# RWKV scan in an encoder kernel: a chunk's state share accumulates in the bank of the passed-on share, and the second direction's decay products move up beside it

## The reference, cut to what matters

```
def step(state, inp):                       # one token; state is 64 x 64 for each head
    r, w, k, v, a, b = inp
    sa = state @ a
    state = state * w + outer(sa, b) + outer(v, k)
    return state, state @ r
out = scan(forward inputs) + flip(scan(flipped inputs))
w = exp(-exp(w_log)),  icl = sigmoid(a0 + ad @ a_up),  w_log = -softplus(-(w0 + wd @ w_up)) - 0.5
```

## Time and profile before

| | us |
|---|---|
| median of 3 runs | 1811.07 (1809.88 to 1813.27) |
| the profiled execution | 1806.79 |
| its span, first to last instruction | 1805.1 |
| TensorE busy with matmuls | 1633.4 |
| VectorE busy | 1235.8 |
| ScalarE busy | 769.1 |
| mean granted TensorE clock, share of full | 0.946 |

### The profile page before, as it was taken

One profiled execution on the slowest core, in us unless ns is written; L12 is line 12 of the kernel. 1 busy time (PEld: TensorE's weight loads), 2 busy tenths in 40 slices (PEclk: granted clock), 3 DMA queues, 4 the chain that ended last, 5 costly groups with the idle time before them and its releaser, 6 DMA issues.

```text
span 1805.1 us, 43648 instructions
## 1 busy us (share of the span) xinstructions
PE 1633.4 (90%) x17117; PEld 1507.3 (84%) x17117; DVE 1235.8 (68%) x1850; ACT 769.1 (43%) x1163; POOL 92.4 (5%) x112
## 2 busy tenths in 40 slices
PE   6999998868878889999999999988688788999999
PEld 6999986757868869999889988867588687899997
DVE  5677667897647556777666777678874665567766
ACT  5444553435232135544444446534342311355444
POOL 1000100001100001000000002000011000010000
PEclk9999998978979989999999999989689799999999
DMA  5755532222102025555556554222220121355555
GB/s 187 263 181 184 173 106 71 94 94 71 38 25 84 27 81 165 178 187 178 189 195 227 187 185 166 94 71 95 70 85 25 36 72 38 102 165 180 187 183 192
DMA packets 62927, 231.58 MB, mean 128 GB/s; under 512 B 7024, under 2 KB 8048, under 8 KB 61840
## 3 DMA queue, kind: packets, MB, share of 16 engines
q1 hardware_dynamic: 61488, 221.41, 36.4%
q0 software_dynamic: 1248, 7.46, 1.1%
HBM read 228.09 MB, written 1.05 MB: 127 GB/s over the span
## 4 chain that ended last, share of the span: by engine, by line
PE 70%; DVE 14%; issue 9%; ACT 5%; DMA 2%; DVEq 0%; ACTq 0%; SPq 0%; POOLq 0%
PE banks L538 14%; PE banks L540 13%; PE banks L539 13%; PE banks L605 9%; PE banks L606 5%; DVE wlo L1407 3%; PE banks L939 2%; DMA raw<-in_stream 2%; DVE cvx L1635 2%; PE banks L937 2%; PE banks L928 1%; PE banks L865 1%; ACT whi L1083 1%; DVE arena L1848 1%; ACT arena L1260 1%
## 5 line engine op out<-in xcount | busy, mean ns | idle before, releaser
L1407 DVE TENSOR_TENSOR wlo<-raw,whi 128x1024 fp32r<-128x1024 f32 x417 | 511.8, 1231 | 327.0 <-ACT whi L1083 325.8
L1083 ACT CAST whi<-raw 128x1024 fp32r<-128x1024 f32 x417 | 435.4, 1048 | 442.4 <-PE banks L540 296.7
L538 PE MATMUL banks<-hx,whi 128*128 128x256 f32 x1696 | 491.9, 290 | 52.5 <-DVE wlo L1407 19.5
L540 PE MATMUL banks<-hx,wlo 128*128 128x256 f32 x1696 | 486.8, 287 | 0.0
L539 PE MATMUL banks<-hx,whi 128*128 128x256 f32 x1696 | 486.7, 287 | 0.0
L538 PEld LDWEIGHTS banks<-hx,whi 128*128 128x128 f32 x1696 | 332.6, 196 | 58.9 <-issue 20.6
L539 PEld LDWEIGHTS banks<-hx,whi 128*128 128x128 f32 x1696 | 332.6, 196 | 0.2
L540 PEld LDWEIGHTS banks<-hx,wlo 128*128 128x128 f32 x1696 | 332.3, 196 | 0.0
L538 PE MATMUL banks<-h,whi 128*128 128x256 f32 x896 | 275.1, 307 | 29.4 <-ACT arena L1180 16.6
L539 PE MATMUL banks<-h,whi 128*128 128x256 f32 x896 | 263.6, 294 | 0.0
L540 PE MATMUL banks<-h,wlo 128*128 128x256 f32 x896 | 262.9, 293 | 0.0
(11 more groups left out here) (293 smaller groups left out, 1888.8 us busy)
## 6 DMA issues: line engine op xcount, KB each, us to landing
raw<-in_stream SPq DMA_DIRECT2D x417, 512.0 KB, 3.3
arena<-in_wuq POOLq DMA_DIRECT2D x2, 1152.0 KB, 11.0
lo_w<-in_lora POOLq DMA_DIRECT2D x2, 1024.0 KB, 7.6
arena<-in_wukv POOLq DMA_DIRECT2D x2, 1024.0 KB, 15.0
xT<-in_x SPq DMA_DIRECT2D x1, 1024.0 KB, 4.9
out<-xT SPq DMA_DIRECT2D x8, 128.0 KB, 3.5
consts<-in_cst SPq DMA_DIRECT2D x1, 642.5 KB, 8.4
vec_t<-in_vecs POOLq DMA_DIRECT2D x3, 113.0 KB, 4.1
```

Source lines behind the costliest of these rows:

```text
L538: TE.matmul(o, wh, hi, start=first, stop=False, **kw)
L540: return TE.matmul(o, wl, hi, start=False, stop=last, **kw)
L1083: SE.copy(whi[:, m % HL, :], raw[:, m % RAW, :]).then_inc(hi_ready, 1)
L1407: TT(wlo[:, m % HL, :], raw[:, m % RAW, :], whi[:, m % HL, :].bitcast(F), ALU.subtract)\
```

## The change

- P and Q are no longer computed for all four chunks in one stage. A new function `local(d, i)` computes them for the chunk of step i alone, for i = 0, 1, 2, in banks 0, 2 and 3. The last chunk's are not computed, nor is the first chunk's P. `local(d, 1)` comes before the filling of point ("o", d), `local(d, 0)` and `local(d, 2)` after it.
- Q stays in its PSUM bank. The product of ptr and the state before (the "state" products) is accumulated on top of it (start=False), and one VectorE instruction over 128 partitions multiplies the sum by the decay into qw. tmp_s and the separate additions are gone.
- "inter" puts odd and even heads into the two halves of one bank, and osum is two instructions of 128 partitions in place of four of 64.
- In direction 0 the second direction's two `lora` products are issued beside the states: column 0 into banks 1 and 4 after `local(0, 2)`, column 1 into banks 0 and 5 after qw of the first chunk. ScalarE does their sigmoids at the same places (`sw`, `icl`), and VectorE does the second direction's scans and subtraction (`decays(1)`) after the qw of i = 1. TensorE's wait for osum moves from `lora` to the transposes.
- The table of fillings: the 8 pieces of ("lora", 1) and 2 of ("kr", 1) go to ("o", 0) (+2), ("state", 0, 1) (+2) and ("state", 0, 2) (+6). The sum is the same. Units 14 to 18 are then due at ("state", 0, 0), ("state", 0, 2) and, as before, ("kr", 1).

```diff
-FILL_R = {"key sums": 8, "key inverse": 8, "values": 8}
+FILL_R = {"key sums": 8, "key inverse": 8, "values": 8, ("lora", 0): 14}
 for _d in range(2):
-    FILL_R.update({("lora", _d): (14, 8)[_d], ("kr", _d): (36, 26)[_d], ("tk", _d): (5, 6)[_d], ("pairs", _d, 0): 9,
-                   ("pairs", _d, 1): (8, 9)[_d], ("x", _d): (8, 6)[_d], ("o", _d): 4})
-    FILL_R.update({("state", _d, i): n for i, n in enumerate((4, 2, 2))})
+    FILL_R.update({("kr", _d): (36, 24)[_d], ("tk", _d): (5, 6)[_d], ("pairs", _d, 0): 9, ("pairs", _d, 1): (8, 9)[_d],
+                   ("x", _d): (8, 6)[_d], ("o", _d): (6, 4)[_d]})
+    FILL_R.update({("state", _d, i): n for i, n in enumerate(((4, 4, 8), (4, 2, 2))[_d])})
...
+            all_members = [m for i in range(2) for q in QUADS for m in members(q)[i::2]]
+            def local(d, i):
+                c, b = STATE_ORDER[d][i], bank[STATE_BANKS[i]]
+                t, e = c // 2, slice(HD * (c % 2), HD * (c % 2) + HD)
+                for n, (x, h, r, j) in enumerate(all_members):
+                    hs = slice(h * HD, (h + 1) * HD)
+                    TE.matmul(b[r:r + HD, j * HD:(j + 1) * HD], tk[e, 2, t, hs], vt[e, t, hs], start=n < 2, stop=False,
+                              skip_group_check=True)
+                for x, h, r, j in all_members:
+                    hs = slice(h * HD, (h + 1) * HD)
+                    m = TE.matmul(b[r:r + HD, j * HD:(j + 1) * HD], tk[e, 1, t, hs], ys[e, x, t, :],
+                                  start=False, stop=i == 0, skip_group_check=True)
+                if i:
+                    for x, h, r, j in all_members:
+                        m = TE.matmul(b[r:r + HD, S + j * C:S + (j + 1) * C], xs[e, x, t, :],
+                                      tk[e, 1, t, h * HD:(h + 1) * HD], start=False, stop=True, skip_group_check=True)
...
+                settled(pe)
+                local(d, 1)
                 fr.at(("o", d))
...
+                pe.wait_ge(*vec.at(("o", d, 0)))
+                settled(pe)
+                local(d, 0)
+                pe.wait_ge(*vec.at(("o", d, 1)))
+                settled(pe)
+                local(d, 2)
+                if d == 0:
+                    lora(1, 0, (1, 4))
+                chunks = STATE_ORDER[d]
                 fr.at(("state", d, 0))
-                pe.wait_ge(*vec.at(("qw", d, 1)))
+                if d == 0:
+                    pe.wait_ge(*vec.at(("qw", d, 0)))
+                    lora(1, 1, (0, 5))
                 for i in (1, 2):
...
-                        m = TE.matmul(bank[h % 2][r:r + HD, j * HD:(j + 1) * HD], ptr[r:r + HD, j, c, :],
-                                      qw[r:r + HD, j, before, :], start=True, stop=True)
+                        m = TE.matmul(bank[STATE_BANKS[i]][r:r + HD, j * HD:(j + 1) * HD], ptr[r:r + HD, j, c, :],
+                                      qw[r:r + HD, j, before, :], start=False, stop=True, skip_group_check=True)
...
                 fr.at(("o", d))
-                for i in range(3):
-                    fr.at(("state", d, i))
+                if d == 0:
+                    sw(1, (1, 4))
+                fr.at(("state", d, 0))
+                if d == 0:
+                    icl(1, (0, 5))
+                fr.at(("state", d, 1))
+                fr.at(("state", d, 2))
...
+                ve.wait_ge(*ten.at(("local", d, 0)))
+                ve.wait_ge(*vec.at(("wch", d)))
+                TT(qw[:, :, chunks[0], :], state(0, 0), decay(0), ALU.mult).then_inc(*vec.mark(("qw", d, 0)))
+                for i in (1, 2):
+                    ve.wait_ge(*ten.at(("local", d, i)))
+                    TT(ptr[:, :, chunks[i], :], one.unsqueeze(1).broadcast_to([P, RC, C]), state(i, S), ALU.subtract)\
+                        .then_inc(*vec.mark(("ptr", d, i)))
                 fr.at(("state", d, 0))
                 for i in (1, 2):
                     ve.wait_ge(*ten.at(("state", d, i)))
...
-                    for e in range(2):
-                        r = HD * e
-                        ve.wait_ge(*vec.at(("decayed", d, i, e)))
-                        TT(qw[r:r + HD, :, c, :], qw[r:r + HD, :, c, :], tmp_s[r:r + HD], ALU.add)\
-                            .then_inc(*vec.mark(("state", d, i, e)))
+                    TT(qw[:, :, chunks[i], :], state(i, 0), decay(i), ALU.mult).then_inc(*vec.mark(("qw", d, i)))
                     fr.at(("state", d, i))
+                    if d == 0 and i == 1:
+                        decays(1)
...
-                for e in range(2):
-                    for g in range(2):
...
+                for g in range(2):
+                    o = osum[:, 2 * g:2 * g + 2, a:z]
+                    m = TT(o, o, bank[2 + g][:, :].rearrange("p (j t) -> p j t", j=2)[:, :, a:z], ALU.add)
```

More of the change, by code:

```diff
@@ L383, in program @@
         QUADS = range(2)
+        STATE_BANKS = (0, 2, 3)
+        STATE_ORDER = [tuple(range(NCH)), tuple(range(NCH - 1, -1, -1))]
         def members(q):
@@ L852, in _, with lora @@
             m.then_inc(*ten.mark("vt"))
+            def lora(d, col, two_banks):
+                for c in range(RC):
+                    m = TE.matmul(bank[two_banks[c // 2]][:, (c % 2) * S:(c % 2 + 1) * S],
+                                  lo_w[HD * d:HD * d + HD, col, c * P:(c + 1) * P],
+                                  wag[HD * d:HD * d + HD, col, :], start=True, stop=True)
+                m.then_inc(*ten.mark(("lora", d, col)))
+            all_members = [m for i in range(2) for q in QUADS for m in members(q)[i::2]]
[14 more added lines that the diff above has]
+                                      tk[e, 1, t, h * HD:(h + 1) * HD], start=False, stop=True, skip_group_check=True)
+                m.then_inc(*ten.mark(("local", d, i)))
             for d in range(2):
-                pe.wait_ge(*act.at("wag"))
                 if d == 0:
+                    pe.wait_ge(*act.at("wag"))
                     pe.wait_ge(*vec.at("kk"))
@@ L860, in _ @@
                     pe.wait_ge(*act.at("nu"))
[L861 to L870, removed]
+                    lora(0, 0, (0, 1))
+                    lora(0, 1, (2, 3))
+                    fr.at(("lora", 0))
                     pe.wait_ge(*vec.at(("conv", *CONV_TAPS[-1][::-1])))
@@ L888, in _ @@
                 pe.wait_ge(*act.at(("sw", d)))
+                if d:
+                    pe.wait_ge(*vec.at(("osum", 0)))
                 for i in range(3):
@@ L1011, in _ @@
                         fr.at(("state", d, 1))
-                        pe.wait_ge(*vec.at(("state", d, 1, 1)))
+                    pe.wait_ge(*vec.at(("ptr", d, 1) if i == 1 else ("qw", d, 1)))
                     settled(pe)
@@ L1330, in _ @@
                 SE.preload_act_table(ACT.Sigmoid)
-                fr.at(("lora", d))
                 if d == 0:
+                    fr.at(("lora", 0))
                     sc.wait_ge(*ten.at("cv mean"))
@@ L1762, in _, with decays @@
             by_tile = lambda a: a.rearrange("p c (t q) -> p c t q", t=NT)
-            for d in range(2):
+            def decays(d):
                 ve.wait_ge(*act.at(("sw", d)))
-                if d == 0:
-                    ve.wait_ge(*vec.at("first values"))
                 for c in range(RC):
@@ L1776, in _ @@
                     conv(len(taps))
+            for d in range(2):
+                if d == 0:
+                    ve.wait_ge(*vec.at("first values"))
+                    decays(0)
                 ve.wait_ge(*act.at(("w", d)))
@@ L1896, in _ @@
                 a, z = (C, S) if d == 0 else (0, S - C)
-                for e in range(2):
-                    for g in range(2):
-                        r = HD * e
-                        o = osum[r:r + HD, 2 * g:2 * g + 2, a:z]
-                        m = TT(o, o, bank[2 + e + 2 * g][r:r + HD, :].rearrange("p (j t) -> p j t", j=2)[:, :, a:z],
-                               ALU.add)
+                for g in range(2):
+                    o = osum[:, 2 * g:2 * g + 2, a:z]
+                    m = TT(o, o, bank[2 + g][:, :].rearrange("p (j t) -> p j t", j=2)[:, :, a:z], ALU.add)
                 m.then_inc(*vec.mark(("osum", d)))
```

74 lines of the change are left out of this document (20 added, 54 removed).

## The result

The changed kernel takes 1789.68 us (median of 4 runs, 1778.93 to 1790.32), the kernel before 1810.47 beside it (4 runs, 1805.63 to 1813.27). The ratio is 0.9875, 95% interval 0.9848 to 0.9903. The profiled execution took 1790.32, its span is 1788.6, 16.5 less than before. The forecast was 1785, from a sum of 25.6 for the two layers. So two thirds of the sum arrived in the profile; by the two medians it is 20.8, for the profiled execution was the slowest of its four. What is missing isn't spread evenly: the hand-over gave about what the sum said, and the end of direction 1 lost time in layer 0 instead of gaining.

The account below looks back on a forecast made before the run. TensorE, busy 90% of the span, bounds the kernel, with VectorE's chain from direction 1's decays setting the hand-over's end. 2 x (10.2 hand-over + 2.6 end of direction 1) = 25.6 us gives 1785; own range 1778 to 1791, 8 in 10 1775 to 1798.

Parts of the forecast that it names:

- Rates: TensorE's `local` products: 0.030 us a record, as column halves overlap by two; bounds 0.018 and 0.059.
- The rival "no overlap": `local` products on TensorE don't overlap, 0.059 a record, 3.7 us more per direction: 1800 us; chance 0.10.
- `lora` at full clock: Hand-over, TensorE: `lora` column 0 at half of 0.45 a record, 1.8 us for 8 records; 3.6 at the lower clock.
- Unit 15's wait: Hand-over: TensorE newly waits 1.5 us for unit 15's add, which stands behind the scans in VectorE's queue.
- kr 9.5 us earlier: Hand-over, VectorE: direction 1's kr starts at 526.7 instead of 536.16, following osum.
- 12.7 at piece 144: Hand-over: TensorE's pieces 144 to 149 start 12.7 us earlier, 3.2 of it since unit 15 leaves the kr-to-bt stretch.
- Clock behind the stand: After TensorE's 6 us stand, lower clock: 18 matmuls take 3.9 us instead of 2.7, transposes lose 1.3; 10.2 a layer remains.
- End of direction 1: Direction 1's state steps and osum shorten, first state products unmoved within 0.3 us: 2.6 us gained a layer, bounds 1.5 and 4.
- The rival of the VectorE queue: VectorE's new order in the hand-over takes back more than 1.5 us, 4 to 5 a layer: about 1794 us; chance 0.14.
- The slower rival: After the 6 us stand TensorE stays at 1.2 GHz up to the next "o", +25 to 30 us a layer: 1841; chance 0.04.
- The short chain: Something else orders kr, leaving only direction 1's 5 us and a few of the hand-over: 1803 us; chance 0.06.
- the clock rival: Same as the slower rival: lower TensorE clock after the hand-over's 6 us stand, 1841 us; chance 0.04.

Follow-up runs that it names:

- e7: e4 with the calls of chunks 1 and 2 of `local` interleaved product by product, in both directions; 1776.07 us, ratio 0.9807 to the kernel before.
- e4: The changed kernel with `local(1, 1)` behind the four pieces of point "o" in direction 1, not ahead of them; 1776.12 us, ratio 0.9842 to the kernel before.
- e1: The changed kernel run again with nothing edited; 1783.89 us, ratio 0.9865 to the kernel before.
- e2: Only the change's state part (`local`, PSUM accumulation, new osum); direction 1's `lora`, sigmoids, scans and fillings as before; 1788.14 us, ratio 0.9908 to the kernel before.
- e5: e4 with six of direction 1's filling pieces moved from ahead of the transposes to behind them; 1776.63 us, ratio 0.9808 to the kernel before.
- e8: e4 with interleaved chunks 1 and 2 of `local` plus twelve unused products in TensorE's stand before piece 144; 1776.36 us, ratio 0.9814 to the kernel before.

## Why the prediction was right, and where a term was off

The time fell inside the forecast's own range, 4.7 above the 1785, by a mechanism that came out step by step in one part and failed in the other. That it fell there is in part luck: the two ends of direction 1 were to give 5.2 us and lost 3.3, and the range was wide enough to hold that. The wider range of 8 in 10 has a slip: its lower bound names 5 us of clock, and 5 us below 1785 is 1780, not 1775.

- **Rates.** `local` at 0.030 a record: measured 0.029. Column halves that share their rows do overlap by two. The rival "no overlap" falls. e7 shows that four quarters take half of that, 0.015. It doesn't show a price of sharing the rows: the diagonal quarters, whose row groups differ, run at 0.030 too, so the rate here goes with the number of quarters in use, two or four. The Trainium skill, "TensorE: Matmul & The Clock Gate", Part 3, says that a weight load is pulled ahead of running matmuls if its row group doesn't conflict or it goes to the background buffer. That one row group keeps the diagonal's rate and isn't at 0.059 agrees with the second condition.
- **`lora` at full clock**: predicted 0.225 a record, measured 1.92 us for 8 (515.45 to 517.37, where the next piece starts), 0.24.
- **Unit 15's wait**: predicted 1.5, measured 0.67 (526.85). The add itself ended 17.8 behind the end of "o", predicted 17.7; TensorE came to it 1.0 later than predicted, since each change from one kind of product to the next took about 0.1 that I hadn't counted (two pieces start 0.12 apart, but the first one behind other products is followed after 0.22: 517.37, 517.59, 517.71).
- **kr 9.5 us earlier**: before, it began 30.74 behind the end of "o" (536.16 - 505.42), after, 21.42 (530.45 - 509.03): 9.3.
- **12.7 at piece 144**: before 45.66 behind the end of "o" (551.08), after 33.02 (542.05): 12.6. The stand is 6.01, predicted 6.
- **Clock behind the stand**: 18 matmuls in 4.02 us, predicted 3.9. The transposes lost 0.2 (2.99 against 2.79), predicted 1.3. Up to the transposes the hand-over gave 11.4 in layer 0 (37.04 us, predicted 37), and with them 11.2 instead of 10.2, within its bounds of 8 and 12.7.
- **Layer 1, the same hand-over**, gave 9.8 us, 1.6 less than layer 0 (from the end of "o" to the transposes before 1401.55 to 1449.85, 48.30; after 1394.78 to 1433.31, 38.53). The forecast took both layers as alike. What differs is a stand of 1.17 us released by "issue" inside "o", after which the pieces run at the lower clock, from 1396.4 to 1399.8. In e4 the stand there is 1.05 us, the clock stays up, and the hand-overs are 41.1 and 41.2 (timeline, TensorE, after):

```profile
1394.48 0.27 PE L1002 MATMUL banks<-arena 64*64 64x64 f32 x2 [1.17 <-issue]
...
1396.37 0.58 PE L540 MATMUL banks<-h,whi 128*128 128x256 f32 x1
```

- **End of direction 1, the step that failed.** The prediction put three `local` calls at 3.85 us in place of 4.0 of "pq", "the first state products come at the same time within 0.3 us", and 2.6 us gained a layer, bounds 1.5 and 4. Measured: 4.4 lost and 1.1 gained. The step that failed is the start of the state products: they come 6.3 and 3.0 us later than before, counted from the first product of "o" (17.62 and 14.00 us against 11.33 and 11.05), not within 0.3. The sum had put TensorE's stand for its instructions, and the clock behind it, at nothing. The rates of `local` were right, but the run of 192 and 48 records with no pieces between stops for 2.54 and 1.91 us, where before it stopped for 1.20 and 0.92, and behind the stop the clock can fall: for 13.7 us in layer 0, for 3.4 in layer 1. In e1 it was down for 13.6 us in layer 0 and not at all in layer 1. With the call four pieces later (e4) the state products come 0.1 us earlier than before in both layers, "inter" 2.7 and 2.6 earlier, as the step said, and the two ends gain 3.0 and 4.1; the sum said 2.6, bounds 1.5 and 4. Put that into the profile of after (26.9 and 22.3 replaced by 19.5 and 19.3) and its 1790.32 becomes 1779.9; the sum said 1781.
- **The rival of the VectorE queue** (1794) didn't occur: `lora` was never at the lower clock. **The slower rival** didn't occur in the hand-over: up to the inverse direction 1 took 20.3 us before and 20.3 after, and the stage behind it 39.2 and 38.8. **The short chain** falls with kr. But the clock rival named the right kind of price at the wrong place: after a stand of 2.5 us the lower level lasted 13.7 us.

## What to carry to other kernels

Between two long runs of small TensorE products leave some wide matmuls; a cost that is right for each product still misses that the run as a whole can outpace what feeds it. A stand released by "issue" costs its own length and sometimes the clock behind it. Look for it in the trace of the kernel before, by its count of instructions: an edit that packs work closer there makes it longer. When the stretches that nobody edited vary by more than the edit is worth, compare segments of the timeline and not totals.

## What the hardware showed that I had not expected

- In two profiles of the changed kernel TensorE stood 2.54, 1.91, 2.15 and 2.30 us at the same record of a run of small products, in e2 2.15 and 2.19; with 12 wide matmuls ahead of it 0.68 and 0.43. All of them end 1.19 to 1.32 us after a packet of instructions has landed.
- The granted clock fell behind stands of 0.95 us (e5) and 1.17 us (after, layer 1), and stayed up behind 0.68 (e4), 0.78 (e7), 0.90 (after, direction 0 of layer 0) and 1.38 us (e8, direction 1 of layer 0). The length of the stand alone doesn't settle it: behind 2.15 us it fell and behind 2.30 it stayed (e1), and behind the 1.20 us stand before, at 617.19, it stayed at 1.00, as the timeline and the windows of the kernel before show:

```profile
617.19 0.27 PE L983 MATMUL banks<-arena 64*64 64x64 f32 x2 [1.20 <-issue]
```

```profile
618.40:621.00 2.60, 2.54 (x98) 2.27 (x96) 1.76 (x5) 1.32 (x2) 0.00 (x0) 1.00 0.02 6
```

- Products with no use, put into a stand, shorten the work behind it: 1.2 and 1.3 us for a stand of 6 us, up to the transposes.
